# The front of a two-block transformer kernel: modulation by quarters of the model width, the first projection by halves of K, and one turn of hidden values placed earlier

## What is computed

```python
mod = silu(c) @ ada_w + ada_b                 # 6 sections of 2048; sections 0 and 1: shift and scale of h1
h1  = rmsnorm(x) * norm1_g * (1 + mod[1]) + mod[0]
proj = h1 @ w_in                              # q_a (512 columns) first, then k_a, v_a, q_c, ...
# four attention mixers on proj, w_out, then 16 experts of width 512, top 2 of a group:
y = sum(combine[:, e] * ((silu(t @ w_gate[e]) * (t @ w_up[e])) @ w_down[e]) for e in range(16))
# second block; its Hyena filters need no token and are computed at the front:
h = sin-MLP(position features) @ filt_w4 * decay ; k = h / sum|h| ; k_f = rfft(k)
```

## Time and profile before

| | us |
|---|---|
| median of 3 runs | 2736.07 (2735.10 to 2736.53) |
| the profiled execution's own time | 2739.57 |
| its span, first to last instruction | 2737.8 |
| PE busy in the span | 2630.7 (96%) |
| DVE busy | 1863.0 (68%) |
| ACT busy | 1305.5 (48%) |
| POOL busy | 102.8 (4%) |
| moved by DMA | 641.18 MB, mean 234 GB/s |

### The profile page before, as it was taken

How to read it: one execution, slowest core, us unless ns; L and a number is a source line. 1 busy time by engine, 2 the same in 40 slices (tenths; PEclk the granted TensorE clock), 3 DMA queues, 4 the chain that set the end, 5 groups by cost and what they waited for, 6 DMA issues and landing times.

```text
span 2737.8 us, 33703 instructions
## 1 busy us (share of the span) xinstructions
PE 2630.7 (96%) x13209; PEld 2171.8 (79%) x13209; DVE 1863.0 (68%) x2427; ACT 1305.5 (48%) x1684; POOL 102.8 (4%) x104
## 2 busy tenths in 40 slices
PE   4699999999999999999999999999999999999998
PEld 2399888777888878787788688888888888888886
DVE  6988857866777888898877765756554554455445
ACT  2345535445445677777543243444444434443443
POOL 1000000000000000000132300000000000000000
PEclk9899999999999999999999999999999999999999
DMA  9997765617777899999454454554555555655553
GB/s 340 383 378 294 279 242 195 222 43 264 262 267 265 318 363 366 359 370 366 182 200 169 154 191 146 196 184 169 188 181 184 187 197 188 195 186 193 191 189 118
DMA packets 179898, 641.18 MB, mean 234 GB/s; under 512 B 11115, under 2 KB 11196, under 8 KB 137000
## 3 DMA queue, kind: packets, MB, share of 16 engines
q1 hardware_dynamic: 171648, 593.53, 61.1%
q0 software_dynamic: 5264, 27.21, 2.8%
q10 hardware_dynamic: 2840, 18.43, 1.8%
HBM read 632.79 MB, written 6.34 MB: 233 GB/s over the span
## 4 chain that ended last, share of the span: by engine, by line
PE 76%; DMA 9%; DVE 8%; ACT 4%; issue 3%; ACTq 0%; SPq 0%; DVEq 0%
PE ps L2082 74%; DMA raw<-in_stream 8%; DVE w_lo L1205 3%; ACT w_hi L684 2%; DVE raw L1281 2%; DMA arena<-in_filt_w 1%; PE ps L2245 1%; PE ps L2736 0%; DVE arena L1782 0%; ACT arena L705 0%; DVE arena L2004 0%; DVE arena L2003 0%; ACT arena L1013 0%; ACT arena L834 0%; DVE arena L1751 0%
## 5 line engine op out<-in xcount | busy, mean ns | idle before, releaser
L1205 DVE TENSOR_TENSOR w_lo<-raw,w_hi 128x1024 fp32r<-128x1024 f32 x968 | 1179.2, 1231 | 679.3 <-ACT w_hi L684 672.3
L684 ACT ACTIVATE w_hi<-raw 128x1024 fp32r<-128x1024 f32 x968 | 1012.6, 1058 | 1037.9 <-PE ps L2082 947.4
L2082 PE MATMUL ps<-w_hi,r_two 128*128 128x512 f32 x2368 | 753.0, 394 | 13.5 <-DVE w_lo L1205 6.0
L2082 PE MATMUL ps<-w_hi,h_two 128*128 128x512 f32 x2432 | 758.9, 391 | 4.5 <-DVE w_lo L1205 2.9
L2082 PE MATMUL ps<-h_two,w_hi 128*128 128x256 f32 (+1 forms) x2048 | 553.0, 343 | 4.3 <-DVE w_lo L1205 3.6
L2082 PEld LDWEIGHTS ps<-w_hi,r_two 128*128 128x128 f32 x2368 | 446.6, 189 | 116.8 <-DVE w_lo L1205 17.9
L2082 PEld LDWEIGHTS ps<-w_hi,h_two 128*128 128x128 f32 x2432 | 456.5, 188 | 102.6 <-DVE w_lo L1205 4.0
L2082 PE MATMUL ps<-w_lo,h_two 128*128 128x512 f32 x1216 | 473.4, 389 | 0.0
L2082 PE MATMUL ps<-w_lo,r_two 128*128 128x512 f32 x1184 | 463.0, 391 | 0.0
L2082 PE MATMUL ps<-h_two,w_lo 128*128 128x256 f32 x1536 | 433.4, 282 | 0.0
L2082 PEld LDWEIGHTS ps<-h_two,w_hi 128*128 128x128 f32 x2048 | 354.1, 191 | 50.5 <-issue 7.4
(11 more groups left out here) (340 smaller groups left out, 1448.7 us busy)
## 6 DMA issues: line engine op xcount, KB each, us to landing
raw<-in_stream SPq DMA_DIRECT2D x516, 1024.0 KB, 5.6
under_r<-in_stream SPq DMA_DIRECT2D x58, 512.0 KB, 6.2
arena<-in_mod_units ACTq DMA_DIRECT2D x16, 1024.0 KB, 5.5
arena<-in_stream SPq DMA_DIRECT2D x25, 512.0 KB, 6.2
under_h<-in_stream SPq DMA_DIRECT2D x13, 512.0 KB, 5.7
filters<-arena POOLq DMA_DIRECT2D x4, 1024.0 KB, 9.6
under_r<-filters POOLq DMA_DIRECT2D x4, 1024.0 KB, 6.2
x<-in_x POOLq DMA_DIRECT2D x1, 2048.0 KB, 37.3
```

What stands on the lines that cost most here:

```text
L684: act.activation(dst, src, ACT.Copy).then_inc(hi_ready, 1)
L1205: dve.tensor_tensor(low, src, high, ALU.subtract).then_inc(lo_ready, 1)
L2082: return pe.matmul(o, a, b, start=start, stop=stop)
```

## The change

- **Order of the 32 units.** `mod_unit(m)` takes four units of shift, then four of scale, for each quarter of the model width, in turn. After every eighth unit DVE forms four columns of `gain` (`gain_ready`). Units 0 to 15 are enough for the K tiles 0 to 7 of h1.
- **The silu(c) row** is loaded by SP ahead of the units instead of by ACT; ACT's queue begins with the filter tables. POOL loads the filter block's operands ahead of the bias tables. DVE starts with the filter MLP, and the first modulation unit comes behind its first layer.
- **Filter blocks with four modulation units** each instead of six; the remaining eleven come behind block 3.
- **a_q by halves of K, in landing places of their own.** The first halves of its four units are loaded into the space of `w_lo` (seen as float32, `under_lo`) behind units 18, 20, 22 and 24; the second halves into `under_r` (`first_late`) ahead of unit 28. PE does the first half (K tiles 0 to 7) of all four units, then tiles 8 to 11 of all four, then 12 to 15, each unit in a bank of its own (0, 1, 2, 7). `raw` is free for a_k's four units, which follow the modulation units directly.
- **h1.** PE's transposes of x are in two parts, before `spectrum(3)` and behind the first half of unit 0, into eight banks. ACT instead of DVE applies gain and shift (`first_out`). The low parts of the first two quarters are POOL's, those of the last two DVE's. The store of filter 3 waits until all 32 units are done, and POOL's narrow load comes behind it.
- **The asides.** The first two can be loaded only when the second halves that lie in their places are used up (`lo_ready` 7 and 8; before, when the 32 units were done). `aside(0)` stands on DVE between `first_lo(6)` and `first_lo(7)`, and asides 5, 6 and 7 stand together ahead of a_k's fourth half.
- **The last expert.** `turn_hidden(15)` goes ahead of the fourth half of `down(14)`, with ACT's and DVE's parts one and two steps later, into a place of its own in `r_hi`, `r_lo` (`hidden_at`).

```diff
+FIRST_AT = (18, 20, 22, 24)
+FIRST_BANKS, FIRST_TURNS = (0, 1, 2, 7), (0, 1, 7, 2, 3, 4, 5, 6)
...
+def mod_unit(m):
+
+    return m // 8 * 4 + m % 4 + m // 4 % 2 * DC
...
+        first_f = at(F_TAPS, DC, T)
+        first_late = under_r[:, 1, :].rearrange("p (s n) -> p s n", s=SLOTS)
...
-                sp.wait_ge(ada_done, FIRST_UNITS - 3 + s)
-                sp.dma_start(raw[:, s, :], sp_units[ADA_UNITS + s]).then_inc(landed[s], 16)
-
+            sp.dma_start(c_row, d["c_row"].partition_broadcast(P)).then_inc(sem("ld_front"), 16)
+            for m in range(FIRST_UNITS):
+                if m >= SLOTS:
+                    sp.wait_ge(ada_done, m - 3)
+                if m == FIRST_UNITS - SLOTS:
+                    sp.wait_ge(sem("rn_ready"), 4)
+                    for j in range(SLOTS):
+                        sp.dma_start(first_late[:, j, :], sp_units[ADA_UNITS + j][:, HALF:UNIT]).then_inc(sem("ld_dft"), 16)
+                sp.dma_start(raw[:, m % SLOTS, :], sp_units[mod_unit(m)]).then_inc(landed[m % SLOTS], 16)
+                if m in FIRST_AT:
+                    j = FIRST_AT.index(m)
+                    sp.dma_start(under_lo[:, j, :], sp_units[ADA_UNITS + j][:, 0:HALF]).then_inc(sem("ld_front"), 16)
...
-                sp.wait_ge(lo_ready, 2 * n - 6)
+                if n < 2 * SLOTS:
+                    sp.wait_ge(ada_done, FIRST_UNITS - 2 * SLOTS + n + 1)
+                else:
+                    sp.wait_ge(lo_ready, 2 * n - 6)
...
+            for n in range(SLOTS, 2 * SLOTS):
+                weight(n)
+            sp.wait_ge(lo_ready, 7)
             aside(0)
+            sp.wait_ge(lo_ready, 8)
             aside(1)
-            weight(4)
             sp.wait_ge(sem("kf_stored1"), 32)
             aside(2)
...
+            for b in range(4):
+                if b == 3:
+                    for q in range(2):
+                        pool.wait_ge(sem("norm_hi"), q + 1)
+                        pool.tensor_tensor(h_lo[:, 4 * q:4 * q + 4, :], first_f[:, 4 * q:4 * q + 4, :],
+                                           h_hi[:, 4 * q:4 * q + 4, :].bitcast(F32), ALU.subtract).then_inc(sem("norm_lo"), 1)
+                pool.wait_ge(sem("spectrum_out"), 4 * b + 4)
+                if b == 3:
+                    pool.wait_ge(ada_done, FIRST_UNITS)
+                pool.dma_start(kf_dram[b], ko[b % 2].rearrange("p a n -> p (a n)")).then_inc(sem(f"kf_stored{b % 2}"), 16)
+            load("ld_narrow", (at(12960, DC, 24), d["w_gate_nsa"]))
             pool.wait_ge(sem("brow_stored"), 16)
...
+            def first_out(q):
+
+                act.wait_ge(sem("norm_t"), 2 * q + 2)
+                act.wait_ge(sem("gain_ready"), q + 1)
+                for c in range(4 * q, 4 * q + 4):
+                    ins = act.activation(first_f[:, c, :], ps[:, FIRST_TURNS[c // 2], c % 2 * T:(c % 2 + 1) * T], ACT.Identity,
+                                         bias=mod[:, c:c + 1], scale=gain[:, c:c + 1])
+                ins.then_inc(sem("norm_f"), 1)
+                act.wait_ge(sem("norm_f"), q + 1)
+                copy(h_hi[:, 4 * q:4 * q + 4, :], first_f[:, 4 * q:4 * q + 4, :]).then_inc(sem("norm_hi"), 1)
+
+            def first_hi(j):
+
+                if j < SLOTS:
+                    act.wait_ge(sem("ld_front"), 16 + 16 * SLOTS)
+                    copy(w_hi[:, j, :], under_lo[:, j, :]).then_inc(hi_ready, 1)
+                else:
+                    act.wait_ge(sem("ld_dft"), 16 + 16 * SLOTS)
+                    act.wait_ge(half_done, j - 3)
+                    copy(w_hi[:, j % SLOTS, :], first_late[:, j % SLOTS, :]).then_inc(hi_ready, 1)
+
             abs_taps(0)
...
-            phase("a_q", heads_out(qT, "q_out", lambda s: 4 + s))
+            for j in range(4, 8):
+                if j == 4:
+                    first_hi(7)
+                else:
+                    hi(0, j + 3)
+                done(0, j)
+                bank = FIRST_BANKS[j - 4]
+                copy(qT[:, 2 * j - 8, :], ps[0:64, bank, 0:T]).then_inc(sem("q_out"), 1)
...
+                if k == LAST_TURN + 1 and p == N_EXP - 1:
+                    hidden_hi(p)
...
+                    if n % 8 == 7:
+                        q = slice(n // 8 * 4, n // 8 * 4 + 4)
+                        dve.wait_ge(mod_ready, n // 4 + 1)
+                        dve.scalar_tensor_tensor(gain[:, q], mod[:, u - 3:u + 1], 1.0, col("norm1", DC)[:, q], ALU.add, ALU.mult)\
+                            .then_inc(sem("gain_ready"), 1)
+
+            def first_lo(j):
+
+                dve.wait_ge(hi_ready, j + 1)
+                src = under_lo[:, j, :] if j < SLOTS else first_late[:, j % SLOTS, :]
+                dve.tensor_tensor(w_lo[:, j % SLOTS, :], src, w_hi[:, j % SLOTS, :].bitcast(F32), ALU.subtract).then_inc(lo_ready, 1)
...
+            def first_low(q):
+
+                dve.wait_ge(sem("norm_hi"), q + 1)
+                dve.tensor_tensor(h_lo[:, 4 * q:4 * q + 4, :], first_f[:, 4 * q:4 * q + 4, :],
+                                  h_hi[:, 4 * q:4 * q + 4, :].bitcast(F32), ALU.subtract).then_inc(sem("norm_lo"), 1)
...
+            for j in range(SLOTS):
+                first_lo(j)
+                modulation(done_units, 1)
+                done_units += 1
+            modulation(done_units, FIRST_UNITS - done_units)
+            dve.wait_ge(sem("norm_lo"), 2)
             dve.sem_inc(ada_done, ADA_UNITS - FIRST_UNITS)
...
+            first_low(2)
+            first_low(3)
...
-            gated_norm_gain(1, "norm1")
...
-            norm_split("h1", (h_hi, h_lo), DC, hf, 0, gain, mod[:, 0:DC], early=first_lo, early_at=11)
-            lo(0, 2)
...
+            for j in range(4, 7):
+                first_lo(j)
+            aside(0)
...
-            phase("a_q")
+            for j in range(4, 8):
+                if j == 4:
+                    first_lo(7)
+                else:
+                    lo(0, j + 3)
+                aside(j - 3)
+            for k in range(5, 8):
+                aside(k)
             phase("a_k")
+            dve.wait_ge(sem("narrow_hi"), 1)
...
@@ -1768,6 +1863,8 @@
                     place_weights()
                 if k == 3 and p:
                     hidden_lo(p - 1)
+                if k == LAST_TURN + 2 and p == N_EXP - 1:
+                    hidden_lo(p)
...
+            def first_part(j, s, first, last):
+
+                for c in range(first, last):
+                    ins = three(ps[:, FIRST_BANKS[s], 0:T], w(j, c % 8 * P, P), H(c), c == 0, c == DC - 1)
+                return ins
...
+            pe.wait_ge(sem("norm_lo"), 2)
+            for j in range(SLOTS):
+                pe.wait_ge(lo_ready, j + 1)
+                first_part(j, j, 0, 8).then_inc(half_done, 1)
+                if j == 0:
+                    first_turn(4, 8)
+            pe.wait_ge(sem("norm_lo"), 3)
+            for j in range(SLOTS, 2 * SLOTS):
+                pe.wait_ge(lo_ready, j + 1)
+                first_part(j, j - SLOTS, 8, 12)
+            pe.wait_ge(sem("norm_lo"), 4)
+            for j in range(SLOTS, 2 * SLOTS):
+                first_part(j, j - SLOTS, 12, 16).then_inc(half_done, 1)
...
+                    if p == N_EXP - 1 and 16 + k == LAST_TURN:
+                        turn_hidden(p)
...
-            turn_hidden(N_EXP - 1)
```

More of the change, by code:

```diff
@@ L122, in norm_count, with hidden_at @@
         n += made[kind]
+LAST_TURN = 19
+def hidden_at(q):
+    return 4 if q == N_EXP - 1 else 0
 FFN_TILES = (16, 16, 12)
@@ L251, in two_blocks @@
         w_hi = sb("w_hi", [P, 4, HALF], F32R)
+        with nc.sbuf_tensor("under_lo", [P, 4, HALF], F32) as under_lo:
+            pass
         w_lo = sb("w_lo", [P, 4, HALF], F32R)
@@ L496, in _ @@
             for k in range(len(ASIDE)):
-                if k % 2 == 0:
+                if k % 2 == 0 and k // 2 + 5 >= 2 * SLOTS:
                     weight(k // 2 + 5)
@@ L670, in _ @@
             pool.wait_ge(sem("cols_added"), 2 + 8)
[L671 removed]
+            load("ld_row", (row, d["norm_final_g"].partition_broadcast(P)))
         @block.scalar
@@ L2197, in _ @@
                     make_taps(b + 1)
+                else:
+                    first_turn(0, 4)
                 spectrum(b)
```

159 lines of the change are left out of this document (75 added, 84 removed).

## The result

The changed kernel takes 2747.39 us (median of 20 runs, 2731.48 to 2752.29), the kernel before 2736.14 us beside it: ratio 1.0035, 95% interval 1.0026 to 1.0044, so 7 to 12 us **slower**. The forecast of 2729.8 had the wrong sign, and its range, to 2738, does not hold the time. The profiled execution spans 2745.6 us, against 2737.8 before. Runs of one kernel mostly lie within 6 us of their median. So the ratios carry the argument, and single profiles show places. Of PE's 107 us of idle time before, only 60 lie in the first 140 us, not all of it as the text ahead of the prediction has it.

A forecast was written before the change was run, and what follows sets the result against it. The front was taken as bound by the DMA weight stream, later stretches by PE. Front -5.3, clock +1.7 and experts -2.7 summed to -6.3 us: 2733.3 for the profiled execution, 2729.8 as the median, range 2722 to 2738.

The forecast's parts named there:

- T: End of the last modulation instruction in the front: 124.64 + 5.0 for more bytes - 1.9 for idle DMA = 127.7 us.
- The asides: DVE's chain of aside loads behind T, landing in 5.0 us: low part 11 ends at T + 36.3 = 164.0 us.
- the -5.3 us: Front's gain at half 11, the first behind a_k's fourth: 164.0 us against PE's 169.3 before.
- TensorE's clock: PE idles some 5 us ahead of half 11, then runs at the lower clock: 1.7 us back, bounds 0 and 3.4.
- GpSimd: Its two low parts in the front might block DVE: taken as 0, upper end 3.6 us.
- rival D: GpSimd's operations hold up two modulation instructions through the shared port: 3.6 us, 2733.4 us; chance 0.06.
- The end of the experts: PE's 3.01 us wait before the last down projection goes, next weight unit then late: 2.7 us gain, bounds 0 and 4.7.
- A: Slower: asides between low parts 6 and 11 on DVE are requested late and land at 7.1 us or later: 2742.7; chance 0.10.
- C: No measurable change: T 5.0 us later, 6 us landings, front gives 0 to 1 us, experts 2.7: 2733; chance 0.24.
- B: More gain: asides 5 to 7 need no wait, T at 125.8, no clock loss, 4.7 at the experts: 2721.7; chance 0.15.
- E: First K halves of a_q not done beside the stream because ACT or DVE are late: 2729; chance 0.03.

The follow-up runs named there:

- e1: Changed kernel with a_q's four first halves issued at modulation units 10, 12, 14, 16 instead of 18, 20, 22, 24; ratio 1.0006 to the kernel before.
- e6: e1 with the four late (second) halves also issued two units sooner, ahead of unit 26 instead of 28; ratio 0.9998 to the kernel before.
- e4: Changed kernel with low parts 0 and 1 of the first projection's input on DVE instead of GpSimd; ratio 1.0046 to the kernel before.
- e2: Kernel before with only the last expert's hidden tile turned, copied and split five halves earlier; ratio 1.0008 to the kernel before.
- the best version: Changed kernel with first and late halves earlier, late halves' places swapped, low part 7 ahead of the first aside, the last expert's turn undone; ratio 0.9980 to kernel before.
- e5: Changed kernel with two counters instead of one for a_q's four first halves, places and order kept; ratio 1.0020 to the kernel before.

## Why the prediction was wrong, step by step

- **T: the step that failed.** "T = 124.64 + 5.0 - 1.9 = 127.7", with "the four `lo` among them cost DVE 4.6 us, which lie beside the landing of the last units". It treated the stretch as a sum of bytes over a rate, with DMA fed throughout. Measured 137.56, 9.9 late. What was missing is DVE's wait of 8.62 us and the 6.1 us of idle DMA behind it. Of the 9.9 e1 gives back 6.8 (the shared counter) and e6 another 2.3 (the late halves issued last, for no reason but their place in SP's order), though the second figure is no larger than the spread of T between profiles; so is the 0.8 left. The bytes fit: with both repaired T is 128.5, and 126.2 in another session. What I did not ask is what DVE's `first_lo(0)` waits for, and what waits for DVE: the wait was on the fourth half, issued at 93.44, while DVE's turn for the first came at 98.3.
- **The asides.** The mechanism was right: landings of 5.21 and 6.86 us, waits of 5.26 and 6.91 on DVE, aside(0) at T + 13.4 (T + 12.7 expected), low part 11 at T + 38.7 (36.3). The second aside landed slower than the 5.0 I took. At half 11 the -5.3 us became +7.0: 9.9 from T and 2.4 from the asides. With the 2.7 of the experts these two make 15.0 of the 15.9 us between the forecast's -6.3 and the 9.6 that the ratio gives.
- **TensorE's clock.** After 4.73 us idle the granted clock was 0.51 and 0.64 in the next 4 us: (0.49 + 0.36) x 2 = 1.7 us of the lower level, as forecast. Not in the sum was PE's idle time of 15.14 us ahead of 143.62; PE waits for low parts again at 153.43 and 162.71, so what the clock costs behind it does not reach half 11.
- **GpSimd.** Taken at 0. The addition into `mod` took 2.18 us instead of 0.16 beside GpSimd's second low part (below), yet e4 shows that the time of the changed kernel does not hang on it. As the cause of this loss rival D falls. The reason given, that the first operation falls where DVE waits anyway, held only by the stall: with the stall gone (e1) the two cost DVE 3.6 us, the upper end of the prediction.
- **The end of the experts.** "2.7 us", bounds 0 to 4.7: measured none in four pairs. The next unit was taken to land 2.4 us behind the last, at 1300.6; in e2 it landed at 1301.95, 11.05 us behind its issue, and by that profile's 2.2 us lead this is 3.6 us later than forecast. The chain of e2 and of the changed kernel runs through that landing to the first column block, and the DMA share is 0.98 to 1.01 from 1290 to 1306 in before and e2. That PE's gap was slack of the stream is my reading of these rows; no run with an earlier landing tests it.
- **The rivals.** A had the sign and two thirds of the size (+6.6 us against +9.6), and named the asides' chain from a late T; its own numbers (T at 129.6, landings of 7.1) were not what happened, so its nearness is luck in part. C, no change, is what one gets once the stall is repaired (e1, e6). B did not come even in the best version: its asides still wait for landings. E did not happen: PE had done the first halves at 128.5, 9 us ahead of T, though ACT and DVE were late with the first of them.
- **"I am wrong if PE is held in the filter blocks so that T moves beyond 130"**: T did, but DVE was held, by ACT and one landing.

## What to carry to other kernels

Ask of every wait that a change puts into the queue of the engine that frees a stream's buffers: which transfer is the last that its counter counts, when is that one issued, and does the stream run dry meanwhile. One counter for four transfers makes the first reader wait for the fourth; here it moved the end of the stream by 7 us. An earlier issue gave 8 us of time back; a second counter gave 7 us of T back too, and some 4 us of time, with intervals that overlap. A gap of the compute engine in a stretch where the DMA engines are at 1.0 may be slack of the stream: removing one of 3.01 us here brought nothing, and the chain went through the next landing. Last, profile the same program twice before reading a shift of 2 or 3 us out of two profiles; the identical front of before and e2 moved by 3.5.

## What the runs showed of the hardware

A DVE instruction of 128x4 that takes 0.16 us took 2.18 while GpSimd worked on two operands in SBUF. GpSimd, changed kernel:

```profile
109.84 2.68 POOL L608 TENSOR_TENSOR h_two<-arena,h_two 128x1024 fp32r<-128x1024 f32 x1 [9.38 <-ACT h_two L740]
```

DVE's row started 0.52 us behind it, at 110.36, and ended with it (112.54 and 112.52). In e5 the same held a modulation instruction for 3.94 us instead of 2.29 and a low part for 2.91 instead of 1.22. It goes the other way too: in e1 a modulation instruction began first, at 101.15, and GpSimd's second low part took 4.24 us instead of 2.35 to 2.7:

```profile
101.40 4.24 POOL L608 TENSOR_TENSOR h_two<-arena,h_two 128x1024 fp32r<-128x1024 f32 x1 [1.25 <-ACT h_two L740]
```

The Trainium skill, page "SBUF — State Buffer", section "SBUF: two separate sides", says that a DVE instruction with two SBUF inputs and a GpSimd operation that reads SBUF exclude each other, and that the one that starts first keeps the port pair for its whole instruction. The rows agree, in both directions, and for an instruction of four columns too. A transfer of 0.5 MB that was queued behind others took 12.34 us to land, against 5.21 on an emptier queue.
